# Window-attention bias added by VectorE, and heads that alternate on two halves of the TensorE array

## The reference, cut to what matters

```
logits = jnp.einsum('bnqkgd,bnjkd->bnkgqj', qb, kb).astype(F32) * (dh ** -0.5) + bias      # window attention
logits = jnp.where(mask, logits, NEG_INF)
m = jnp.maximum(jnp.max(logits, axis=-1, keepdims=True), sink)
p = jnp.exp(logits - m)
probs = p / (jnp.sum(p, axis=-1, keepdims=True) + jnp.exp(sink - m))
...
logits = (jnp.einsum('bqhd,bkhd->bhqk', qn, k_nope)                                       # latent attention
          + jnp.einsum('bqhr,bkr->bhqk', qr, k_rope)).astype(F32) * scale
```

## Time and profile before

| | |
|---|---|
| median of 3 runs | 1442.28 us (1441.08 to 1443.1) |
| the profiled execution: its span, first to last instruction | 1438.6 us |
| PE busy | 1225.2 us, 85% |
| DVE busy | 608.4 us, 42% |
| ACT busy | 218.3 us, 15% |
| HBM | 475.67 MB read, 332 GB/s over the span |
| mean granted TensorE clock | 0.916 |

### The profile page before, as it was taken

One profiled execution on the slowest core, in us unless ns is written; L12 is line 12 of the kernel. 1 busy time (PEld: TensorE's weight loads), 2 busy tenths in 40 slices (PEclk: granted clock), 3 DMA queues, 4 the chain that ended last, 5 costly groups with the idle time before them and its releaser, 6 DMA issues.

```text
span 1438.6 us, 16146 instructions
## 1 busy us (share of the span) xinstructions
PE 1225.2 (85%) x6743; PEld 574.1 (40%) x6743; DVE 608.4 (42%) x1283; ACT 218.3 (15%) x466; POOL 14.6 (1%) x31
## 2 busy tenths in 40 slices
PE   8999999999999999987677877777887777886877
PEld 4785564565885543232222222222232222222223
DVE  4969999678553452323122231222121321222122
ACT  4311012373012411110000100000000100000001
POOL 4000000000000000000000000000000000000000
PEclk9999999999999999999787999898787979788898
DMA  9443352622547579999999999999999999999997
GB/s 302 148 156 133 136 205 110 217 69 88 175 176 271 224 286 424 421 433 433 429 434 427 431 431 430 431 432 431 430 431 430 432 430 429 433 430 432 430 425 301
DMA packets 62728, 478.83 MB, mean 333 GB/s; under 512 B 13573, under 2 KB 21125, under 8 KB 45376
## 3 DMA queue, kind: packets, MB, share of 16 engines
q1 hardware_dynamic: 61392, 477.44, 80.5%
q0 software_dynamic: 864, 0.25, 0.2%
q10 hardware_dynamic: 400, 0.10, 0.0%
HBM read 475.67 MB, written 2.11 MB: 332 GB/s over the span
## 4 chain that ended last, share of the span: by engine, by line
PE 55%; DMA 34%; DVE 5%; ACT 4%; issue 1%; SPq 0%; DVEq 0%; ACTq 0%
DMA ring<-in_moe_w_up_dram 20%; DMA late_ring<-in_moe_w_up_dram 13%; PE bank L726 12%; PE bank L1263 10%; PE bank L1298 7%; PE bank L1028 5%; PE bank L740 4%; PE bank L1284 3%; PE bank L1222 2%; PE bank L1148 2%; PE bank L1019 2%; PE bank L1335 1%; PE bank L1104 1%; PE bank L788 1%; PE bank L710 1%
## 5 line engine op out<-in xcount | busy, mean ns | idle before, releaser
L1263 PE MATMUL bank<-ring,x_gathered 128*32 128x512 f32 x1184 | 253.6, 685 | 55.1 <-DMA late_ring<-in_moe_w_up_dram 35.9
L1263 PE MATMUL bank<-late_ring,x_gathered 128*32 128x512 f32 x800 | 202.9, 684 | 37.0 <-DMA ring<-in_moe_w_up_dram 35.6
L2647 DVE TENSOR_TENSOR tokens_out<-tokens_out,bank 128x512 f32<-128x512 f32 x240 | 148.6, 681 | 192.8 <-PE bank L1335 192.8
L726 PE MATMUL bank<-ring,hT 128*128 128x512 f32 (+2 forms) x448 | 170.3, 541 | 3.4 <-ACT hT L1535 2.6
L2630 DVE SCALAR_TENSOR_TENSOR hidden<-hidden,bank 128x128 f32<-128x128 f32 x31 | 8.9, 288 | 348.5 <-ACT hidden L1850 348.5
L1263 PEld LDWEIGHTS bank<-ring,x_gathered 128*32 128x32 f32 x1184 | 66.7, 124 | 145.8 <-issue 143.9
L1222 PE MATMUL bank<-x_tok,select 128*32 128x512 f32 x512 | 115.9, 1033 | 7.3 <-DVE select L2539 4.2
L726 PEld LDWEIGHTS bank<-ring,hT 128*128 128x128 f32 x448 | 84.7, 190 | 85.7 <-issue 74.0
L1298 PE MATMUL bank<-ring,hidden 128*32 128x512 f32 x560 | 87.1, 778 | 18.2 <-DVE hidden L2632 18.2
L1335 PE MATMUL bank<-y_slots,weight_slots 32*128 32x512 f32 x496 | 72.3, 653 | 29.5 <-ACT y_slots L1865 21.7
L1263 PEld LDWEIGHTS bank<-late_ring,x_gathered 128*32 128x32 f32 x800 | 53.1, 124 | 110.2 <-issue 107.7
(11 more groups left out here) (454 smaller groups left out, 1243.8 us busy)
## 6 DMA issues: line engine op xcount, KB each, us to landing
ring<-in_moe_w_up_dram SPq DMA_DIRECT2D x19, 4096.0 KB, 40.3
ring<-in_moe_w_down_dram SPq DMA_DIRECT2D x16, 4096.0 KB, 29.5
ring<-in_moe_w_gate_dram SPq DMA_DIRECT2D x16, 4096.0 KB, 38.4
late_ring<-in_moe_w_down_dram SPq DMA_DIRECT2D x13, 4096.0 KB, 29.3
late_ring<-in_moe_w_gate_dram SPq DMA_DIRECT2D x12, 4096.0 KB, 39.2
late_ring<-in_moe_w_up_dram SPq DMA_DIRECT2D x10, 4096.0 KB, 38.2
ring<-in_w_in_dram SPq DMA_DIRECT2D x20, 1024.0 KB, 8.6
ring<-in_w_out_dram SPq DMA_DIRECT2D x16, 1024.0 KB, 5.6
```

Of the source, the lines that this page charges most:

```text
L726: mm = pe.matmul(b, lhs(i)[:, P * tt:P * tt + P], piece_view(key)[:, c, at:at + cols], start=i == 0, stop=i == n - 1)
L1263: mm = pe.matmul(gu_bank[SLOTS * c:SLOTS * c + SLOTS, :], XGT[:, at, n % 4, n // 4, :], pieces[c % 2][:, FF * (n % 8):FF * (n % 8) + FF], ...
L2647: ins = v.tensor_tensor(y, x, mix[c][:, :], ALU.add)
```

## The change

The bias is no longer multiplied in by PE. DVE adds it while it takes the score banks from PSUM to SBUF (`add_bias`, L2333 of the new kernel), six adds of 128x512, so ACT's six drains of those banks go too. The table BT has its queries in reverse order; so the queries are now stored in reverse when ACT drains "sqT", and the transposed probabilities are stored in reverse again ("backwards") so that the outputs come out in order. The task list moves "gs1" ahead of the second block's scores, and swaps "sl11" and "sl12".

Scores of two banks, one on each half of the array's rows, are issued in turn; so are the heads of a window output (two halves of the columns). The rope parts of two latent heads now lie on two halves of the partitions (`turned_pairs`), with the shared rope key on both, and the latent scores issue them in turn; "ml0" becomes two banks of half the width.

```diff
-    t += [..., "gs3", "sl00", "sl01", "sl10", "sl11", "gs1", "sl12", "sl13", "sp00", "sp01"]
+    t += [..., "gs3", "sl00", "sl01", "gs1", "sl10", "sl12", "sl11", "sl13", "sp00", "sp01"]
...
-            def window_scores(name, n, places):
+            def window_scores(n, names, firsts):
                 w = P * (n + 1)
-                b = fill(name, cols=len(places) * w)
-                pe.matmul(b.rearrange("p (h w) -> p h w", w=w), const("flip"),
-                          BT[:, places[0]:places[0] + len(places), P * (1 - n):], start=True, stop=False)
-                for i, at in enumerate(places):
-                    h = HEAD_AT[at]
-                    r = slice(64 * (h % 2), 64 * (h % 2) + 64)
-                    mm = pe.matmul(b[:, w * i:w * i + w], SQT[r, h // 2, P * n:P * n + P], SKT[r, h // 4, 0:w],
-                                   start=False, stop=i == len(places) - 1)
-                filled(mm)
+                count = 4 if n == 0 else 2
+                banks = [fill(name) for name in names]
+                for i in range(count):
+                    for b, first in zip(banks, firsts):
+                        h = HEAD_AT[first + i]
+                        r = slice(64 * (h % 2), 64 * (h % 2) + 64)
+                        mm = pe.matmul(b[:, w * i:w * i + w], SQT[r, h // 2, P * n:P * n + P], SKT[r, h // 4, 0:w],
+                                       start=True, stop=True)
+                        if i == count - 1:
+                            filled(mm)
...
+            def turned_pairs(name, src):
+                b = fill(name, cols=2 * P)
+                for i in range(2):
+                    for d in range(2):
+                        mm = pe.matmul(b[64 * d:64 * d + 64, P * i:P * i + P], src(i, d), ident, start=True, stop=True)
+                filled(mm)
...
-            pe.wait_ge(s["band_in"], 32)
+            window_scores(0, ("sl00", "sl01"), (0, 4))
+            pe.wait_ge(s["og_sq"], 2)
+            row_sum("gs1", SUM1)
             for i in range(2):
-                window_scores(f"sl0{i}", 0, range(4 * i, 4 * i + 4))
-            for i in range(4):
-                if i == 2:
-                    pe.wait_ge(s["og_sq"], 2)
-                    row_sum("gs1", SUM1)
-                window_scores(f"sl1{i}", 1, (2 * i, 2 * i + 1))
+                window_scores(1, (f"sl1{i}", f"sl1{i + 2}"), (2 * i, 2 * i + 4))
...
-                    pe.matmul(o, QNT[:, h, q], KNT[:, h, 0:w], start=True, stop=False)
-                    mm = pe.matmul(o, QRT[0:64, h, q], KRT[0:64, 0:w], start=False, stop=True)
+                    for b, h in zip(banks, (2 * i, 2 * i + 1)):
+                        pe.matmul(b[:, w * i:w * i + w], QNT[:, h, q], KNT[:, h, 0:w], start=True, stop=False)
+                    for b, r in zip(banks, (slice(0, 64), slice(64, 128))):
+                        mm = pe.matmul(b[:, w * i:w * i + w], QRT[r, i, q], KRT[r, 0:w], start=False, stop=True)
...
             root_mean_square("gs3", RG2[:, 3, :])
-            for i in range(2):
-                drain(f"sl0{i}", SL0[:, 512 * i:512 * i + 512])
+            task[0] += 2
+            wait_turn(act, "gs1")
+            root_mean_square("gs1", RG2[:, 1, :])
             act.wait_ge(s["sink_in"], 1)
             st.link(nc.scalar.activation(SM[:, 256:264], SM[:, 256:264], ACT.Exp))
             exps(SL0, 8, P, 0, "sl_exp")
-            for i in range(4):
-                if i == 2:
-                    root_mean_square("gs1", RG2[:, 1, :])
-                drain(f"sl1{i}", SL1[:, 512 * i:512 * i + 512])
-            drain("sp00", PT0[:, 0:512])
+            task[0] += 4
+            wait_turn(act, "sp00")
+            def backwards(b):
+                return four(4)(b)[:, :, ::-1]
+            drain("sp00", four(4)(PT0[:, 0:512]), backwards)
...
+            dve.wait_ge(s["band_in"], 32)
+            add_bias("sl00", 0, 0, SL0)
+            add_bias("sl01", 0, 4, SL0)
             wait_task(dve, "sl01")
             window_maximum(0, SL0)
+            for i in range(2):
+                add_bias(f"sl1{i}", 1, 2 * i, SL1)
+                add_bias(f"sl1{i + 2}", 1, 2 * i + 4, SL1)
+            wait_task(dve, "sl13")
+            window_maximum(1, SL1)
             group_scale(3)
             window_normalise(0, SL0)
-            wait_task(dve, "sl13")
-            window_maximum(1, SL1)
             group_scale(1)
             window_normalise(1, SL1)
```

More of the change, by code:

```diff
@@ L202 @@
 HEAD_AT = [2 * (i % 4) + i // 4 for i in range(SWA_H)]
+LATENT_AT = [2 * (i % 2) + i // 2 for i in range(MLA_H)]
 ROW = {}
@@ L952, in _ @@
             key_turned("qnT", lambda tt: [MQ[:, tt, QK_D * h:QK_D * h + NOPE] for h in range(MLA_H)])
-            key_turned("qrT", lambda tt: [MQ[:, tt, QK_D * h + NOPE:QK_D * h + QK_D] for h in range(MLA_H)], parts=64)
+            for tt in range(TT):
+                turned_pairs(f"qrT{tt}", lambda i, d: MQ[:, tt, QK_D * (2 * i + d) + NOPE:QK_D * (2 * i + d) + QK_D])
             pe.wait_ge(s["mkv_n"], 1)
             key_turned("knT", lambda tt: [MKV[:, tt, 256 * h:256 * h + NOPE] for h in range(MLA_H)])
-            transposes("krT", [CKV[:, tt, 256:320] for tt in range(TT)], parts=64)
+            turned_pairs("krT", lambda tt, d: CKV[:, tt, 256:320])
             wait_task(pe, "sp01")
@@ L1680, in _ @@
             for tt in range(TT):
-                drain(f"sqT{tt}", SQT[:, :, P * tt:P * tt + P], four(4), scale=SM[:, 152:153])
+                drain(f"sqT{tt}", SQT[:, :, P * tt:P * tt + P], lambda b: four(4)(b)[:, :, ::-1], scale=SM[:, 152:153])
             drain("skT", SKT[:, :, :].rearrange("p v (t q) -> p t v q", t=TT),
@@ L1705, in _ @@
             for tt in range(TT):
-                drain(f"qrT{tt}", QRT[0:64, :, P * tt:P * tt + P], four(4), parts=64)
+                drain(f"qrT{tt}", QRT[:, :, P * tt:P * tt + P], four(2), cols=256)
             for tt in range(TT):
                 drain(f"knT{tt}", KNT[:, :, P * tt:P * tt + P], four(4), scale=col("mla_kn_nope_g"))
-            drain("krT", KRT[0:64, :], cols=T, parts=64)
+            drain("krT", KRT[:, :], cols=T)
             act.wait_ge(s["sink_in"], 2)
@@ L1716, in _ @@
             mla_scale = float(QK_D) ** -0.5
-            drain("ml0", L0[:, 0:512], scale=mla_scale)
-            drain("ml10", L0[:, 512:1024], scale=mla_scale)
-            drain("ml11", L0[:, 1024:1536], scale=mla_scale)
+            for i in range(2):
+                drain(f"ml0{i}", L0[:, 256 * i:256 * i + 256], cols=256, scale=mla_scale)
+            for i in range(2):
+                drain(f"ml1{i}", L0[:, 512 * i + 512:512 * i + 1024], scale=mla_scale)
             for i in range(4):
-                drain(f"sp1{i}", PT1[:, 512 * i:512 * i + 512])
+                drain(f"sp1{i}", four(4)(PT1[:, 512 * i:512 * i + 512]), backwards)
             act.wait_ge(s["ml_max"], 1)
@@ L2310, in latent_normalise, with add_bias @@
                 normalise(latent[n], MLA_H, P * (n + 1), 4 * n, "ml_p")
+            def add_bias(name, n, first, scores):
+                heads = 4 if n == 0 else 2
+                w = P * (n + 1)
+                wait_turn(dve, name)
+                wait_filled(dve, name)
+                v.tensor_tensor(scores[:, w * first:w * first + 512].rearrange("p (h w) -> p h w", w=w),
+                                bank[TASK_NO[name] % 8][:, :].rearrange("p (h w) -> p h w", w=w),
+                                BT[:, first:first + heads, P * (1 - n):], ALU.add).then_inc(s["psum_drained"], 1)
+            dve.wait_ge(s["band_in"], 32)
+            add_bias("sl00", 0, 0, SL0)
+            add_bias("sl01", 0, 4, SL0)
             wait_task(dve, "sl01")
             window_maximum(0, SL0)
+            for i in range(2):
+                add_bias(f"sl1{i}", 1, 2 * i, SL1)
+                add_bias(f"sl1{i + 2}", 1, 2 * i + 4, SL1)
+            wait_task(dve, "sl13")
+            window_maximum(1, SL1)
             group_scale(3)
             window_normalise(0, SL0)
-            wait_task(dve, "sl13")
-            window_maximum(1, SL1)
             group_scale(1)
             window_normalise(1, SL1)
-            wait_task(dve, "ml0")
+            wait_task(dve, "ml01")
             latent_maximum(0, latent[0])
```

43 lines of the change are left out of this document (21 added, 22 removed).

## The result

| | before | after |
|---|---|---|
| median of 12 runs each | 1440.09 us | 1446.24 us |
| lowest to highest | 1438.24 to 1443.1 | 1443.56 to 1446.9 |
| ratio, 95% interval | | 1.0039 (1.0030 to 1.0047) |
| span of the profiled execution | 1438.6 us | 1444.7 us |

The changed kernel is slower by 0.39%, some 5.6 us (4.3 to 6.8 by the interval; 6.2 between the medians); the predicted shift of 6.6 lies inside, near its upper end. The two profiled executions differ by 6.1 us. In the one after, VectorE reaches the window softmax 0.48 us later than in the one before (300.46 against 299.98, a difference that is already there at 255 us); where a stage time is given less the start, that is taken off.

What follows compares the result with a forecast made beforehand. At the change, DVE's order was taken to delay the first normalise, with ACT and PE waiting; +3.3 without the clock and +3.3 for it gave +6.6, so 1448.9 us (own spread 1446.5 to 1451.5; range 1442.0 to 1453.0).

Steps and rivals of the forecast that it cites:

- rival 1: Attention stage: PE's idle costs nothing through the granted clock, so only +3.3, 1445.6 us; chance 0.16.
- The first normalise: DVE's window softmax: six adds, second maximum and group scale come first, so it ends at 314.63, not 308.03: +6.6.
- ACT up to krT: ACT's drains behind the first transposes: sp00's drain starts +5.1, two shorter rope-query drains give -0.45, krT ends +4.65.
- The table load: ACT's load ahead of the second sink exponential goes: -1.28, leaving the second normalise +3.35 late.
- The clock: PE's 11.5 us idle brings half speed: 2.3 at the first transposes, 1.0 later, together +3.3, ends 0 and +5.2.
- The second, taken at 1.0: PE idles 4 us between latent scores and second normalise; a low stretch would cost 1.8 to 2.6, 1.0 taken.
- The tail: From 324 us on, transposes, so1 and latent parts: so1's saving mostly runs into a wait, -0.05, ends 0 to -0.4.
- Passing on: From 324 us PE leads without slack to the experts, so the shift reaches the end at full size.
- The lasting low level: PE at 0.50 for 13.6 us through both groups loses 6.8: +10.1, 1452.4 us; chance 0.10.
- Absorption at the queue: SP queue: experts' transfers start at 538 us as before and PE's waits absorb the delay: 1442.3, no change; chance 0.10.
- ACT as the limit: Window softmax: first normalise follows ACT's exponentials at once, giving -2.2, 1440.1 us or a little faster; chance 0.10.
- The last rival: PE's array halves do not overlap: no shift of the sum, 1448.9 us; counted in the forecast, no separate chance.

Runs made afterwards that it cites:

- the run with PE kept busy: Changed kernel plus nine 128x512 products on PE between the last window score and the first transposes: 1444.08 us, ratio 1.0023.
- the turns in the idle: Changed kernel with latent transposes ahead of window scores, key transposes and latent scores in PE's idle, second exponentials and first normalise earlier: 1437.69 us, ratio 0.9979.
- the run with the normalise early: Changed kernel with the first normalise on VectorE right behind the adds, ahead of the second maximum and first group scale: 1439.25 us, ratio 0.9995.
- with PE kept busy besides: Changed kernel with the first normalise right behind the adds and four 128x512 products in PE's idle: 1437.93 us, ratio 0.9978.
- first normalise later: Changed kernel with the second group scale also ahead of the first normalise on VectorE: 1449.72 us, ratio 1.0058.
- group scale behind: Changed kernel with the first group scale moved behind the first normalise, the second maximum still ahead of it: 1440.42 us, ratio 0.9999.
- gs1 moved alone: Kernel before with only gs1's sum and square root moved ahead of the second block's scores: 1440.80 us, ratio 0.9992.

## Why the prediction was right, and where its steps were off

**The number.** The time of 1446.24 lies 2.7 us below the 1448.9 of the forecast, just outside its own spread and next to the 1445.6 of rival 1. Most of that is the base: 1442.28 was a median of three runs, and twelve runs of the same kernel give 1440.09. So the time alone could not tell the forecast from rival 1. The shift (5.6 to 6.2 us, where rival 1 has 3.3) and the run with PE kept busy do.

**The first normalise** held: +6.7 measured, +6.6 in the sum. Six adds, the second maximum and the group scale have the lengths taken from the earlier trace rows, the adds 0.72 each with their gap, and VectorE has no idle among them. The waits that move along cost nothing in the changed kernel, as reasoned, but not by much: PE stood 4.60 us ahead of gs1's sum and was done with the scores at 304.74, not near 303, and in the runs with PE kept busy and without the alternation the adds waited 0.26 for its banks.

**ACT up to krT** was taken too short. Without the clock the second block's transposes came 4.15 late (the run with PE kept busy, above); the sum had 3.35 at that point. There the first normalise ended 0.3 later than the sum had it (its adds waited 0.26 for a bank); the first drain started 0.84 behind the normalise (316.05), where the sum had 0.6; and the nine drains took 4.26 (to 320.31) where it had 4.02. That makes 0.8, of which 0.2 is that run's own wait for a bank; 0.6 is left for the changed kernel.

**The table load** left with its 1.28, as the trace before showed, and with the 0.17 by which the activations stand closer, which the 4.26 above already counts: the sink exponential starts 0.26 behind the start of krT's drain in the changed kernel too (322.70, 322.96). The figure of the Trainium skill's page "ScalarE: Activation LUTs" (section "What ACT_TABLE_LOAD costs"), 2.66 us with its drain, is not borne out on this path by any run here.

**The clock** was the one term of which no row of that stage existed. The first low stretch was there, as forecast, and cost 2.66 where the sum took 2.3 with 1.8 to 2.6 as its ends, so just past them. The second, taken at 1.0, did not come: the latent scores began later and lasted longer than guessed (324.27 to 329.75, guessed 321.6 to 325.8), so PE idled 1.39 us before the next transposes and not 4. That is the step that was wrong in kind. Whether the shorter idle is the reason is not shown: with the turns in the idle the level fell right behind an idle of 1.87 us. Low in two terms (0.6 and 0.4) and high in two others (1.0 here, 0.25 in the tail), the sum came out at 6.6 against 6.3 in the trace at gs0 (343.63 against 336.87, less 0.48). The second normalise ended at 331.08, 330.6 less the start, a tenth past the latest that was forecast. The path is shown; that the errors along it cancel so nearly is luck.

**The tail** gave 0.3, within its ends: the chain from the second normalise to gs0 took 12.55 us instead of 12.85, and so1's shorter time did run into a wait of 0.89 us for the second latent softmax.

**Passing on.** The shift reached the end, but not in every run at its full size. In the run with the normalise early the stage is 0.9 us later than before at the projection (440.19 against 439.28), and still the span is 1.3 us shorter. The products with the experts' down weights on the chain, before and then in that run, show one place where that arises:

```profile
551.19 5.34 PE bank L1298 x32
...
573.58 3.69 PE bank L1298 x32
```

```profile
552.37 3.64 PE bank L1309 x32
...
573.06 3.69 PE bank L1309 x32
```

The first of them takes 5.34 in one and 3.64 in the other, the second 3.69 in both, and the next two agree to 0.05. In the kernel after, the second takes 6.38. The same work thus has several lengths, by where the low clock falls among the experts: the granted clock over these products was 0.68 for the 5.34, 1.00 for the 3.64 and 0.57 for the 6.38. A stage's shift of 1 us can be read from the trace; the time of the whole can't be worked out from it to better than a microsecond or two.

**The rivals.** That the clock plays no part fell with the run that kept PE busy. The lasting low level did come, in the length of its row: 0.50 from 307.4 to 320.9, 13.5 us. But its price was wrong: PE worked in only 5.6 us of that, and the cost was 2.66, where the rival had halved the whole stretch to 6.8 (and passed over the 2.71 us of work in 705.2 to 713.5). Absorption at the queue fell by the landmarks. ACT as the limit fell with VectorE's rows; the run with the normalise early is about that case, made by hand, and it is the kernel before's equal; with PE kept busy besides, it is 0.22% faster (3.2 us, where the rival had 2.2), so there it was the clock that took the gain away. The last rival, halves that do not overlap, was priced wrongly: without the alternation the stage would be 2 us later, not unmoved.

## What to carry to other kernels

Work that is taken from an engine in the middle of a chain and given to another is paid for where the second engine stands in its own order: look at what is queued behind the new instructions there, and put what others wait for first (here one line moved ahead of a maximum and a group scale was worth 6 to 7 us of 1446). Price an idle of TensorE twice, as a wait and as slow work afterwards, and look for work that can fill it. A saving on an engine that then waits (ACT's six drains, 8.3 us of idle) is worth nothing until what it waits for is moved too.

## What was not expected of the hardware

The time at the low clock after PE resumed was 2.6, 3.6, 5.2 and 5.6 us in four runs whose idles were between 4.67 and 13.94 us, and not in the order of the idle: the longest idle (13.94, first normalise later) had the least work in it. In all four the level fell between 307.3 and 308.1 us; it rose at 314.9 and 314.7 in two (normalise early, group scale behind) and at 320.9 and 321.3 in the others, so in these four executions the cost of the idle depended on where in the low stretch PE resumed. The length of the idle does not settle whether the level falls: the first 4.0 us without PE work at 677.2 in the kernel before were at 1.00, while with gs1 moved alone it fell behind an idle of 1.61 us (0.50 in 301.0 to 304.2), and with the turns in the idle behind one of 1.87 us (0.50 in 311.2 to 324.6).

Passes of two heads that alternate on the two halves take less time: the 32 of so1 took 1.97 instead of 3.33 us (338.30 in the run without alternation), the latent scores 5.5 instead of 8.3.
